# A decoder layer on one core: first projections taken from x before its norm, with ones made on the chip and constants loaded after x

## The reference, cut to what matters

```python
def rmsnorm(x, w):
    y = xf * lax.rsqrt(jnp.mean(xf * xf, axis=-1, keepdims=True) + EPS)
    return (y * w.astype(jnp.float32)).astype(x.dtype)
...
q, k, v, g, f_lr, z, xbc, dt_raw = jnp.split(xn @ w_in, offs, axis=-1)      # xn = rmsnorm(h, norm1_w)
gk = (jax.nn.log_sigmoid((f_lr @ w_gk2 + b_gk2)) / GLA_TAU)
dt = jax.nn.softplus(dt_raw + dt_bias)
```

## Time and profile before

| | us |
|---|---|
| median of 3 runs | 2124.3 |
| lowest, highest | 2109.77, 2129.03 |
| the profiled execution | 2123.39 |
| its span in the trace | 2121.2 |
| mean granted TensorE clock, as a share of full speed | 0.974 |

### The profile page before, as it was taken

One profiled execution on the slowest core, in us unless ns is written; L12 is line 12 of the kernel. 1 busy time (PEld: TensorE's weight loads), 2 busy tenths in 40 slices (PEclk: granted clock), 3 DMA queues, 4 the chain that ended last, 5 costly groups with the idle time before them and its releaser, 6 DMA issues. The chain is left out here.

```text
span 2121.2 us, 31685 instructions
## 1 busy us (share of the span) xinstructions
PE 2028.3 (96%) x12559; PEld 1848.1 (87%) x12559; DVE 1209.6 (57%) x2223; ACT 623.0 (29%) x971; POOL 1132.3 (53%) x697
## 2 busy tenths in 40 slices
PE   5999998699899999999999999998999999999996
PEld 3578777577799999999999999997999999999995
DVE  2325364733699787778433332113577777777773
ACT  2224112310242323232323333223333333333331
POOL 0023220200447788888888888884566666666200
PEclk8999998879999999999999999999999999999998
DMA  3097102011235565556555555777999999999961
GB/s 145 2 341 263 40 31 85 1 66 62 94 103 125 124 125 124 125 124 132 127 130 125 124 117 125 157 181 239 325 317 322 320 319 320 321 318 318 328 199 46
DMA packets 231787, 365.34 MB, mean 172 GB/s; under 512 B 92129, under 2 KB 157170, under 8 KB 231026
## 3 DMA queue, kind: packets, MB, share of 16 engines
q1 hardware_dynamic: 153330, 294.43, 42.2%
q0 software_dynamic: 78336, 69.25, 16.6%
HBM read 290.21 MB, written 73.38 MB: 171 GB/s over the span
## 5 line engine op out<-in xcount | busy, mean ns | idle before, releaser
L801 PE MATMUL bank<-xh,usp 128*128 128x288 f32 x4320 | 754.4, 296 | 1.4 <-DVE xl L1429 1.4
L1659 POOL DMA_INDIRECT gates_scratch<-gate_val,gate_at x384 | 667.4, 1738 | 133.8 <-issue 115.8
L896 PE MATMUL bank<-W,vsp 128*128 128x448 f32 x3072 | 636.6, 369 | 9.2 <-DVE W L1558 9.2
L801 PEld LDWEIGHTS bank<-xh,usp 128*128 128x128 f32 x4320 | 636.7, 189 | 3.2 <-DVE xl L1429 1.9
L896 PEld LDWEIGHTS bank<-W,vsp 128*128 128x128 f32 x3072 | 577.8, 188 | 67.8 <-issue 9.4
L801 PE MATMUL bank<-xl,usp 128*128 128x288 f32 x2160 | 462.5, 296 | 0.0
L801 PEld LDWEIGHTS bank<-xl,usp 128*128 128x128 f32 x2160 | 348.0, 189 | 0.0
L1441 DVE TENSOR_TENSOR usp<-ring,usp 128x1024 fp32r<-128x1024 f32 x120 | 146.6, 1222 | 335.0 <-ACT usp L1052 334.7
L1553 DVE TENSOR_TENSOR vsp<-ring,vsp 128x1024 fp32r<-128x1024 f32 x128 | 156.8, 1226 | 177.1 <-ACT vsp L1137 176.7
L1681 POOL DMA_INDIRECT picked<-in_v,row_index x128 | 150.1, 1173 | 193.5 <-DVE acc L1572 167.8
L1078 ACT ACTIVATE gl<-bank 128x288 f32<-128x288 f32 x256 | 91.3, 409 | 522.0 <-PE bank L801 521.7
(11 more groups left out here) (245 smaller groups left out, 1590.0 us busy)
## 6 DMA issues: line engine op xcount, KB each, us to landing
ring<-in_u SPq DMA_DIRECT2D x128, 512.0 KB, 3.7
ring<-in_v SPq DMA_DIRECT2D x128, 512.0 KB, 5.4
hidden_scratch<-gl SPq DMA_DIRECT2D x128, 288.0 KB, 2.2
xn<-hidden_scratch SPq DMA_DIRECT2D x128, 224.0 KB, 5.7
G<-gates_scratch SPq DMA_DIRECT2D x120, 224.0 KB, 4.7
gates_scratch<-zero SPq DMA_DIRECT2D x32, 768.0 KB, 8.9
ring<-in_wproj SPq DMA_DIRECT2D x36, 512.0 KB, 3.8
gates_scratch<-gate_val,gate_at POOLq DMA_INDIRECT x384
```

What stands on the lines that cost most here:

```text
L801: mm = pe.matmul(bank[b + y][:, 0:PHALF], w, src[:, k, y * PHALF:(y + 1) * PHALF], start=(k == 0 and w is hi and src is xh), stop=(k == KT ...
L896: mm = pe.matmul(bank[(k + 4) % 8][:, 0:TA], w, W[:, n % 4, z, :], start=(n == 0 and w is hi and z == 0), stop=(n == NE - 1 and w is lo))
L1659: pool.indirect_dma_start(gates_flat, bass.IndirectOffsetOnAxis(ap=gate_at[0:r, i, x:x + 1], axis=0), gate_val[0:r, i, hh, x - hh * TOPK:x ...
```

## The change

- `ones` and `eps` are tiles of their own, filled by DVE at the start (`ones_ready`), and no more part of `cst`, which becomes 129 columns narrower. ACT and PE wait for `ones_ready` in place of `const_loaded`. The wait for `cst` stands only where the identity is first needed.
- SP issues `prm` first, then x, `small`, `row`, `wgk`, and `cst` behind them.
- DVE writes x·weight without the factor to `mix` (free at this time) as each tile of x lands (`raw_ready`). The small projections and the values read `mix`.
- The reciprocal of the root is taken in `root(0)`, and the factor is applied where the small projections are copied out, now by DVE in place of ACT. DVE then writes `xn` as before, in `norm(0)`.
- PE turns the factor to tokens on partitions by five small matmuls into bank 4, which DVE copies to `rtok`; ACT's copy of each value tile takes it as its scale.
- PE computes the values of token tile 0 right behind the small projections, ahead of the turning of `fl`, and the other four tiles behind the gate's logits, in banks 3, 0, 1, 2.
- The first four projections wait for `normed` before each of their first 8 matmuls.
- Several semaphores are merged into counters (`fl_step`, `gvar_step`, `hsm_keys_loaded`), in the same order of events.

```diff
 # SP
+            sp.dma_start(prm[:, :], d["param"]).then_inc(prm_loaded, 16)
             for k in range(KT):
                 sp.dma_start(h[:, k, :], d["xT"][:, k, :]).then_inc(x_loaded[k], 16)
+            sp.dma_start(small[:, :, :], d["wsmall"]).then_inc(small_loaded, 16)
+            sp.dma_start(row[:, :], d["rows"]).then_inc(small_loaded, 16)
+            sp.dma_start(wgk[:, :], d["w_gk2"]).then_inc(small_loaded, 16)
             sp.dma_start(cst[:, :], d["const"]).then_inc(const_loaded, 16)
-            sp.dma_start(prm[:, :], d["param"]).then_inc(const_loaded, 16)
-            ... (row, small, wgk)
 # PE
-            pe.wait_ge(const_loaded, 32)
+            pe.wait_ge(ones_ready, 1)
...
-                        pe.wait_ge(normed, norm_base[0] + k + 1)
-                    mm = pe.matmul(bank[x][0:DT_ROW + SH, 0:HALF], small[:, k, :], xn[:, k, x * HALF:(x + 1) * HALF],
+                        pe.wait_ge(raw_ready, k + 1)
+                    mm = pe.matmul(bank[x][0:DT_ROW + SH, 0:HALF], small[:, k, :], mix[:, k, x * HALF:(x + 1) * HALF],
...
+            def values(i, b):
+                for k in range(KT):
+                    mm = pe.matmul(bank[b][0:rows(i), :], mix[:, k, cols(i)], wv_sb[:, k, :], start=(k == 0), stop=(k == KT - 1))
+                mm.then_inc(v_done, 1)
+            pe.wait_ge(wv_loaded, 16)
+            values(0, 2)
+            pe.wait_ge(fl_step, 3)
+            for i in range(TILES):
+                mm = pe.matmul(bank[4][0:rows(i), i:i + 1], sq[0:1, 0, cols(i)], ones[0:1, 0:1], start=True, stop=True)
+            mm.then_inc(rtok_ready, 1)
+            pe.wait_ge(const_loaded, 16)
...
+            values(1, 3)
+            values(2, 0)
+            values(3, 1)
+            pe.wait_ge(v_copied, 1)
+            values(4, 2)
...
             for n in range(4):
-                project(n, xn)
+                project(n, xn, norm=0)
 # ACT
-            act.wait_ge(const_loaded, 32)
+            act.wait_ge(ones_ready, 1)
-            act.wait_ge(fl_done, 1)
-            for x in range(2):
-                act.activation(fl[:, x * HALF:(x + 1) * HALF], bank[x][0:DT_ROW + SH, 0:HALF], ACT.Copy).then_inc(fl_copied, 1)
...
+            act.wait_ge(rtok_ready, 2)
             for i in range(TILES):
                 act.wait_ge(v_done, i + 1)
-                act.activation(V[0:rows(i), i, :], bank[2 + i % 2][0:rows(i), :], ACT.Copy).then_inc(v_copied, 1)
+                act.activation(V[0:rows(i), i, :], bank[[2, 3, 0, 1, 2][i]][0:rows(i), :], ACT.Copy,
+                               scale=rtok[0:rows(i), i:i + 1]).then_inc(v_copied, 1)
 # DVE
-            dve.wait_ge(const_loaded, 32)
+            dve.memset(eps, EPS)
+            dve.memset(ones, 1.0).then_inc(ones_ready, 1)
...
+            dve.wait_ge(prm_loaded, 16)
+            for k in range(KT):
+                dve.wait_ge(x_loaded[k], 16)
+                dve.tensor_scalar(mix[:, k, :], h[:, k, :], pp("norm1")[:, k:k + 1], None, ALU.mult).then_inc(raw_ready, 1)
+            root(0)
+            dve.wait_ge(fl_step, 1)
+            for x in range(2):
+                half = slice(x * HALF, (x + 1) * HALF)
+                dve.tensor_tensor(fl[:, half], bank[x][0:DT_ROW + SH, 0:HALF], sq[0:DT_ROW + SH, 0, half], ALU.mult).then_inc(fl_step, 1)
             norm(0)
+            dve.wait_ge(rtok_ready, 1)
+            dve.tensor_copy(rtok[:, 0:TILES - 1], bank[4][:, 0:TILES - 1])
+            dve.tensor_copy(rtok[0:rows(TILES - 1), TILES - 1:TILES], bank[4][0:rows(TILES - 1), TILES - 1:TILES]).then_inc(rtok_ready, 1)
```

More of the change, by code:

```diff
@@ L130, in constants @@
     parts = {
-        "ident": np.eye(P), "ones": np.ones((P, P)),
+        "ident": np.eye(P),
         "incl_a": le & same_a, "incl_b": le & same_b, "suf_a": gt & same_a, "suf_b": gt & same_b,
@@ L138, in constants @@
         "iota": np.tile(np.arange(NK), (P, 1)), "iota16": np.tile(np.arange(TOPK), (P, 1)),
-        "eps": np.full((P, 1), EPS),
         "column": np.stack([peer_cols(i).start + r for i in range(TILES)], axis=1),
@@ L171, in build @@
         cst = sb(base, "cst", [P, CONST_N])
+        ones_sb = sb(base, "ones_sb", [P, P])
+        eps_sb = sb(base, "eps_sb", [P, 1])
+        rtok = sb(base, "rtok", [P, TILES])
         zero = sb(base, "zero", [P, 1, TS // 2])
@@ L183, in pp @@
             return prm[:, a:b]
-        ident, ones = cc("ident"), cc("ones")
+        ident, ones, eps = cc("ident"), ones_sb[:, :], eps_sb[:, :]
         bank = [base.enter_context(nc.psum_tensor(f"bank{n}", [P, 512], F32)) for n in range(8)]
@@ L570, in _ @@
                 pe.matmul(out, ones[0:1, 0:rows(i)], row[0:1, :], start=False, stop=True).then_inc(gk_done, 1)
-            pe.wait_ge(wv_loaded, 16)
-            for i in range(TILES):
-                if i >= 2:
-                    pe.wait_ge(v_copied, i - 1)
-                for k in range(KT):
-                    mm = pe.matmul(bank[2 + i % 2][0:rows(i), :], xn[:, k, cols(i)], wv_sb[:, k, :],
-                                   start=(k == 0), stop=(k == KT - 1))
-                mm.then_inc(v_done, 1)
+            values(1, 3)
[3 more added lines that the diff above has]
+            values(4, 2)
             pe.wait_ge(gk_ready, 1)
-            pe.wait_ge(dtl_copied, 1)
+            pe.wait_ge(fl_step, 5)
+            pe.wait_ge(rtok_ready, 2)
             for p in range(NP):
@@ L1015, in _ @@
             act.activation(gsq, mix[:, 0:GH, :], ACT.Square).then_inc(gsq_ready, 1)
-            act.wait_ge(gvar_ready, 1)
-            act.activation(gstat[:, 0, :], gstat[:, 0, :], ACT.Sqrt).then_inc(groot_ready, 1)
+            act.wait_ge(gvar_step, 1)
+            act.activation(gstat[:, 0, :], gstat[:, 0, :], ACT.Sqrt).then_inc(gvar_step, 1)
             conv_out(7)
@@ L1165, in link, with root @@
                 dve.wait_ge(chain, linked[0])
+            def root(m):
+                for y in range(2):
+                    dve.wait_ge(root_ready, 2 * m + y + 1)
+                    rstd = sq[:, 0, y * HALF:(y + 1) * HALF]
+                    link(dve.reciprocal(rstd, rstd))
             def norm(m):
@@ L1170, in norm @@
                 dst = mix if m == 1 else xn
-                for y in range(2):
-                    dve.wait_ge(root_ready, 2 * m + y + 1)
-                    rstd = sq[:, 0, y * HALF:(y + 1) * HALF]
-                    link(dve.reciprocal(rstd, rstd))
+                if m > 0:
+                    root(m)
                 w = pp(norm_par[m])
@@ L1318, in _ @@
             dve.tensor_scalar(gstat[0:rows(4), 0, 4 * GH:], bank[4][0:rows(4), 4 * GH:5 * GH], 1.0 / DV, EPS, ALU.mult,
-                              ALU.add).then_inc(gvar_ready, 1)
-            dve.wait_ge(groot_ready, 1)
-            dve.reciprocal(gstat[:, 1, :], gstat[:, 0, :]).then_inc(grstd_ready, 1)
-            dve.wait_ge(gbc_done, 1)
+                              ALU.add).then_inc(gvar_step, 1)
+            dve.wait_ge(gvar_step, 2)
+            dve.reciprocal(gstat[:, 1, :], gstat[:, 0, :]).then_inc(gvar_step, 1)
+            dve.wait_ge(gvar_step, 4)
             for hh in range(GH):
```

50 lines of the change are left out of this document (25 added, 25 removed).

## The result

The changed kernel took 2108.4 us, the median of 14 runs (2095.3 to 2114.4), against 2118.3 us for the kernel before in the same comparison (14 runs, 2109.4 to 2129.7). The ratio is 0.9938 with a 95% interval of 0.9913 to 0.9962: faster by 13.1 us of 2118.3 (8 to 18 us), a little over half a per cent. It is not the quotient of the medians: these lie 9.9 us apart, and the means 13.0 us (2119.0 and 2105.9). The forecast was 14.0 us won and 2110 us. The profiled execution after took 2112.5 us with a span of 2110.6 us; the one before had 2123.4 us.

A forecast was written before the change was run, and what follows sets the result against it. The prediction took TensorE's waits and slow clock in the front, before the projections at 94.57 us, as what counts; 6.5 + 8.1 + 0.8 - 0.9 - 0.5 = 14.0 us won from a 2124.3 us median gave 2110 us, range 2098 to 2121.

The forecast's parts named there:

- Part 1: Kernel start: first square and matmul wait for x and a memset, not prm; first matmul at 6.7 us, minus 6.5 us.
- Part 2: Small projections follow the sums without waiting for the norm: 5.71 us rest and 2.4 us slow clock gone, minus 8.1 us.
- Part 3: Value tile 0 behind the small projections hides TensorE's 0.80 us rest during the copy of fl, minus 0.8 us.
- Part 4: Added work: five matmuls turning the factor, plus 0.9 us; fulfilled waits in the projections nothing, at most 4 us.
- Part 5: Gate's logits unchanged at 10.4 us; later clock rises at two places in the front cost plus 0.5 us.
- the rival that had it staying up: Clock stays up through the logits after dense work: 3.9 us more won, 2106 us; chance 0.15.
- The sum: Whole kernel: 6.5 + 8.1 + 0.8 - 0.9 - 0.5 = 14.0 us won, median after 2110 us.
- a microsecond won before 94.57 us is a microsecond of the whole: Front before the 20 projections: nothing later starts at a fixed time, so its gain reaches the end in full.
- a stage after 95 us that grew: Sign of being wrong: any stage behind the front, after 95 us, becoming longer.
- The slower rival: From 350 to 450 us TensorE's clock changes fall anew; mean 0.60 costs 23 us, giving 2133 us; chance 0.04.
- VectorE as the bound of the front: VectorE late by 3 us, waits in the projections costing 4 us, or both: some 5 us lost, 2115 us; chance 0.14.
- The joint of GpSimd and TensorE: Ahead of the last stage: gain given back if GpSimd's gate additions do not move with the front, 2124 us; chance 0.05.

The follow-up runs named there:

- start_only: Kernel before, with only ones and eps written by VectorE and the loads reordered; median 2109.4 us against 2115.6 us, ratio 0.9977.
- start_undone: Changed kernel with the old load order, ones and eps written behind the landing of constants and parameters; projections start at 88.5 us, 8.5 us later.
- value_back: Changed kernel with value tile 0 moved behind the gate's logits with the others; projections start at 85.9 us (80.0 us with the change).
- one_wait: Changed kernel with one TensorE wait on the written xn before the projections in place of 32; their first 128 instructions lasted 32.13 us.
- before_again: The kernel before, unedited, profiled a second time; 2115.7 us.
- weave: Changed kernel with value tile 1 computed between the second and third tile of logits; projections start at 73.3 us, 6.7 us before the change's.
- value_back_xn_late: Changed kernel with value tile 0 behind the logits and VectorE writing xn behind the logits' copies; projections start at 81.2 us.
- after_again: The changed kernel, unedited, profiled a second time; 2103.5 us.

## Why the prediction was right

Point by point, in its own parts:

- **Part 1**, the start, minus 6.5 us. Measured 6.75 us in the profile after, 6.9 us in start_only and 6.6 us in start_undone. x's tile released ScalarE at 4.32 us where 4.60 was reckoned. The mechanism stood as written: table load, square, matmul, in that chain. The square began 0.01 us after the load of 1.28 us ended, so the rule of the Trainium skill, "ScalarE: Activation LUTs", section "What ACT_TABLE_LOAD costs", that a switch also costs a drain of about 1.4 us, again finds no such time in this trace. VectorE's x times weight ended at 11.1 us, inside the sums, and cost nothing.
- **Part 2**, the small projections, minus 8.1 us. The rest of 5.71 us is gone and the 32 take 8.17 us (8.05 reckoned, 10.41 before). They end at 24.6 us, predicted 25.1. Right in both halves: 5.7 us of wait and 2.2 us of clock.
- **Part 3**, the value tile over the copy of `fl`, minus 0.8 us. The number came out, since the two engines were indeed level (31.5 us and 31.6 us, 32.0 predicted). But the sentence that the tile hides the 0.80 us ahead of L562 was wrong as an account of what the tile does. value_back shows its worth as 5.9 us: without it TensorE waits 6.37 us for VectorE, whose `xn` now stands between the copy of `fl` and the dt chain by the same change. The prediction saw the `xn` in that queue only as a risk of 0 to 3 us on top. The cost that the change makes (6 us of `xn` between the copy of `fl` and what TensorE's logits wait for) and the gain that pays it were netted without being named, and the forecast held because both were in the sum by their level ends.
- **Part 4**, plus 0.9 us for turning the factor: measured 0.7 us (31.62 to 32.32). Nothing for the fulfilled waits: shown, 32.13 us for 128 instructions with 32 waits (start_undone) and with one (one_wait), both at full clock. The upper bound of 4 us is out.
- **Part 5**, logits nothing, clock plus 0.5 us. From the turning of `fl` to the values 10.39 us (32.32 to 42.71), 10.4 before. The clock fell in the logits, so the rival that had it staying up did not come. It came back 4.4 us into the values, and in 3.5 us before: 0.45 us lost at half speed. The granted clock changed at other moments in the two executions of one kernel (before and before_again, 20.2 and 24.1 us for the same stretch at 366 to 392 us). The Trainium skill, "TensorE: Matmul & The Clock Gate", Part 1, says that the watch on activity runs freely beside the kernel, so that the point of change varies; these repeats agree in that it varies, and do not test why.
- **The sum.** The front won 14.57 us in the profile, 14.0 forecast; the whole 13.1 us (8 to 18), or 9.9 us by the medians. That the median after, 2108.4 us, lies so near to 2110 us is in part luck: the forecast set out from 2124.3 us, the median of three runs, and the fourteen have 2118.3 us, from which 14.0 us would have led to 2104.3 us. Part 1 gave 0.25 us more, the sums of squares 0.25 us and part 4 0.2 us, part 2 0.1 us less; the repeats of the two kernels differ by 15.5 us (96.1 less 80.6). The step "a microsecond won before 94.57 us is a microsecond of the whole" held within what these runs can tell: at the last stage 10.4 us of 14.6 and 12.5 us of 15.5 were left, and 3.8 us of the first shortfall are a fall of the clock that a second profile of the kernel before has too. "Later stages should all stand 14 us earlier" did not come, and one sign of being wrong, a stage after 95 us that grew, did: the turning of xc to the SSD part, from 20.2 to 24.0 us.
- **The slower rival** described that loss correctly, in the right stretch (350 to 450 us) and by the right cause, a clock that falls in other moments. It was mis-sized: 3.8 us where it put 23 us. Its guess that this is luck of one run fits the kernel before, which had it in one of two profiles; the changed kernel had it in both.
- **VectorE as the bound of the front** did not happen with the tile in place, and happens at once without it (85.9 us). With the tile there was more room than the level ends suggest: behind `xn` VectorE rests 1.32 us and then 0.47 us for TensorE, so `xn` could have ended some 1.8 us later without holding up the logits (an estimate from these two rests; no run tried it). Nobody should move that tile without moving `xn`.
- **The joint of GpSimd and TensorE** passed on what came to it, 9.6 us of distance against 9.5 us, and GpSimd was the later one, as the prediction had it.

## What to carry to other kernels

When a change moves work on two engines at once, write down each move with its own sign before netting them: here one value tile was worth 5.9 us against one block of writes, and moving the block away without the tile 4.7 us, where the net alone said 0.8. A rest of TensorE in front of an engine that is busy elsewhere is a place for independent matmuls, and these can pay more than the rest, since the low clock that comes with such a stretch is paid again in the work behind it (weave: 6.7 us won where TensorE had rested for 2.3 us). Whether the rest or the narrow matmuls around it bring the clock down these runs do not tell apart: in value_back_xn_late it fell in 26 to 28 us (0.76), where the one rest of note was 1.08 us. For effects of ten microseconds in two milliseconds compare the starts of stages in repeated profiles, not whole times: a pace of the last stage that has nothing to do with the edit moves the end by 12 us.

## What the hardware showed that was not expected

- **Two paces of one stage at the same granted clock.** The last stage (3072 matmuls of 448 columns) lasts 624.0 to 625.4 us or 636.5 to 637.6 us, whole executions at one or the other, with the same instructions, TensorE busy throughout and the clock at 1.00. Both kernels showed both. The cause is open; nothing in the rows of TensorE, its waits or the granted clock tells the two apart but the length of the instructions (median 365 ns and 368 ns).
- **The same stretch at two clocks.** The turning of xc up to the SSD part (30 transposes with rests of about 1 us, then 32 matmuls of 128 columns) takes 20.2 to 20.3 us or 23.6 to 24.1 us, by whether the clock falls in it. After and after_again fell, before did not, before_again did.
- **A start at half pace that the clock column does not show.** The first sums run at 0.49 us an instruction and then at about 0.25 us, with the granted clock at 1.00 in both. The change of pace came 2.6 us behind the first matmul in after, 3.6 us in before and 5.6 us in before_again and start_undone.
- **Fulfilled waits are free.** 32 waits on a semaphore long at its value, one for each of 32 matmuls of 296 columns, made no difference that the 0.01 us of the rows can show, in 32.13 us.
- **Copies with a scale.** ScalarE's copy of a value tile with the factor as its scale took 0.67 to 0.69 us, and 0.60 us without, off the path here.
